# A two-layer hybrid trunk on one core: low halves of the first projection's weights moved from GpSimd to VectorE

## The chip, the cores and the metric

The kernel runs on one core of one Trainium2 chip. TensorE (PE) multiplies matrices, VectorE (DVE), ScalarE (ACT) and GpSimd (POOL) compute element by element, and SyncE (SP) issues the transfers. Each engine works through its own instructions in order; semaphores tie the engines together. The metric is the device time of one execution in microseconds (us).

## The reference

272 tokens (16 learned ones and 256 of input) with 1024 features go through two layers. Each layer is

```
h = x + W_out @ concat[ attention | RWKV-7 | convolution ]( RMSNorm(x) @ W_in )
x = h + PEER( RMSNorm(h) )
```

W_in has 2304 columns: 768 for the attention, 1024 for RWKV, 512 for the convolution. The RWKV part first mixes each token with the one before it (the token shift), and the convolution part is a gate and a depthwise filter of 31 taps:

```
prev = pad(z[:, :-1]);  z = z + (prev - z) * mu          # token shift
r, k, v, hw, ha, hg = split(z)
kk = k * k_k;  kk = kk * rsqrt(max(sum(kk * kk), 1e-12))
u = zc[..., :256] * sigmoid(zc[..., 256:])               # convolution's gate
u = conv(u, conv_w, 31 taps) + conv_b
```

PEER scores 128 x 128 experts by two sets of keys, keeps the top 16 of each head, and sums gated rows of two large tables (u and v, 16384 rows each).

## The kernel before, in words

**Weights in two halves.** All large products run in three passes for accuracy. A weight tile (128 x 1024, f32, 512 KB) is loaded by SP, copied by ACT to a rounded high half (`high`, L573), and the low half, weight minus high half, is computed by POOL (`low`, L495) or, for the v table alone, by DVE (L1548). TensorE then multiplies x_hi by w_hi, x_lo by w_hi and x_hi by w_lo (`tile`, 24 products). Tiles of a layer are numbered through: 0 to 17 the first projection (NZ = 18), 18 to 25 the output projection (NOUT = 8), 26 to 41 the query projection of PEER, then 128 tiles of u and 128 of v. Four slots (WR) form a ring: tile n can be loaded when TensorE has used tile n - 4, and ACT makes the high half of n + 2 (AHEAD) just before it waits for tile n to be used (`evacuate`).

**First projection.** Tile n of it gives 128 columns of z for all 272 tokens, and ACT copies them from PSUM (L597). Tiles 0 to 7 are RWKV's, 8 to 11 the convolution's, 12 to 17 the attention's. After tile 11 TensorE does six small products (the LoRAs) between tiles 11 and 12, for which it needs ACT's tanh and sigmoid of the token-shifted chunks 6 and 7; ACT then applies the gates (L653 to L662). The last of these, L662, releases the convolution.

**POOL's order in a layer** is written out: low halves up to tile 19 (`lows(l, 0 or 2, 20)`), then the convolution (one product L512, then 31 taps: two tensor_scalars L516 each, and an addition L525 from the second tap on), then low halves 20 to the end of u and the first two of v, and at last tiles 0 and 1 of the next layer.

**DVE's order in a layer:** the norm (`norm`), the token shift of eight chunks when tile 7 is evacuated (two operations each, L1269 and L1270), kk (L1279) and its square (L1280, the first request to TensorE), the decay (L1283), ten scans (L1288), L1290 to L1298, and L1300, which carries the second request to TensorE. TensorE answers both behind the projection, in order (`asked`), then runs 48 warm-up products on zeros, waits for the third request (L1318) and starts the transposes for the RWKV recurrence. Behind this come the recurrence and the attention, interleaved, and L1396, the request that ends them; TensorE waits for the convolution (`s_conv`) after it.

Of the kernel before, what the change touches and what calls it, by code (L numbers as in the profile page):

```python
# [26 lines left out]
ALU = mybir.AluOpType  # L27
ACT = mybir.ActivationFunctionType
AX = mybir.AxisListType
F32 = mybir.dt.float32  # L30
# [4 lines left out]
D = 1024  # L35
# [4 lines left out]
DEPTH = 2  # L40
# [6 lines left out]
NZ = 18  # L47
# [32 lines left out]
WR = 4  # L80
# [4 lines left out]
NW = NV0 + NKEYS  # L85
NP = NV0 + AHEAD
NLV = NW - NP
OHT = 4
UB = 4
PEEL = 2 * UB  # L90
# [113 lines left out]
def trunk(nc, h0, vec, res_c, mix_c, lora_c, keys_c, w_c, u_c, v_c, out):  # L204
    with ExitStack() as ctx:
# [9 lines left out]
        def sem(name):  # L215
            return ctx.enter_context(nc.semaphore(name))
# [135 lines left out]
        s_hi = sem("weights_high_ready")  # L352
        s_lo = sem("weights_low_ready")
        s_lv = sem("v_weights_low_ready")
        s_use = sem("weight_tile_used")
        s_sq = sem("squares_ready")
        s_ss = sem("square_sums_ready")
# [125 lines left out]
        @block.gpsimd  # L483
        def _(pool):
            nc.gpsimd.memset(zero_t[:, :], 0.0).then_inc(s_zero, 1)
            g = nc.gpsimd
            link = Link(pool, s_gl)

            def low(l, n, it=0):

                at = (l * NW + n) % WR * D
                slot = slice(at, at + D)

                pool.wait_ge(s_hi, l * NW + n + 1 + WR * it)  # L494
                g.tensor_tensor(wlo_t[:, slot], wraw_t[:, slot], whi_t[:, slot].bitcast(F32),  # L495
                                ALU.subtract).then_inc(s_lo, 1)

            def lows(l, n0, n1):

                whole = (n1 - n0) // WR  # L500
                with pool.Fori(0, whole) as it:  # L501
                    for j in range(WR):
                        low(l, n0 + j, it)
                for n in range(n0 + whole * WR, n1):
                    low(l, n)

            for l in range(DEPTH):
                lows(l, 0 if l == 0 else AHEAD, NZ + AHEAD)

                pool.wait_ge(s_cg, 2 * (l + 1))  # L510
                link(g.memset(cu[:, :, 0:CPAD], 0.0))
                link(g.tensor_tensor(cu[:, :, CPAD:CPAD + T], z[:, ZCU:ZCU + 2, 1:T + 1], cacc[:, :, :], ALU.mult))  # L512
                for k in range(CONV_K):
                    for j in range(2):
                        dst = cacc if k == 0 else ctmp
                        ins = g.tensor_scalar(dst[:, j, :], cu[:, j, k:k + T], vcol(l, "conv_w", j * CONV_K + k),  # L516
                                              vcol(l, "conv_b", j) if k == 0 else None, ALU.mult,
                                              *((ALU.add,) if k == 0 else ()))
                        if j == 0:
                            ins.then_inc(s_gl, 1)  # L520
                            link.n += 1
                        else:
                            link(ins)
                    if k:
                        ins = g.tensor_tensor(cacc[:, :, :], cacc[:, :, :], ctmp[:, :, :], ALU.add)  # L525
                        link(ins) if k < CONV_K - 1 else ins.then_inc(s_conv, 1)
                lows(l, NZ + AHEAD, NP)
                if l < DEPTH - 1:
                    for n in range(AHEAD):
                        low(l + 1, n)  # L530


        @block.scalar
# [246 lines left out]
        def _(pe):  # L780
# [21 lines left out]
            def tile(l, n, out_of, hi_of, lo_of, it=0):  # L802


                slot = (l * NW + n) % WR

                if n < NP:
                    pe.wait_ge(s_lo, l * NP + n + 1 + WR * it)
                else:
                    pe.wait_ge(s_lv, l * NLV + n - NP + 1 + WR * it)  # L810
                for c in range(DC):
                    for k, (a, b) in enumerate(((whi, hi_of), (whi, lo_of), (wlo, hi_of))):
                        last = mm(out_of(c), a[:, slot, c, :], b(c), c == 0 and k == 0, c == DC - 1 and k == 2)
                last.then_inc(s_use, 1)
# [70 lines left out]
            for l in range(DEPTH):  # L885
# [234 lines left out]
                def output(i, it=0):  # L1120
# [3 lines left out]
                    slot = (l * NW + n) % WR  # L1124

                    if n < NP:
                        pe.wait_ge(s_lo, l * NP + n + 1)
                    else:
                        pe.wait_ge(s_lv, l * NLV + n - NP + 1 + WR * it)
                    ah, al_ = act_hi[:, i % UB, 0:L.nt], act_lo[:, i % UB, 0:L.nt]  # L1130
# [17 lines left out]
        def _(dve):  # L1148
# [52 lines left out]
            def attention(l):  # L1201
# [23 lines left out]
                for n, s, q, nk, _ in groups(l):  # L1225
# [30 lines left out]
                    v.tensor_tensor(pr, pr, bc(rd, 2, nk), ALU.mult).then_inc(s_tn, 1)  # L1256
                    yield

            for l in range(DEPTH):
                if l == 0:  # L1260
                    dve.wait_ge(s_h, 48)
                L = LAYERS[l]
                norm(l, 0)
                dve.wait_ge(s_mix, 32 * (l + 1))
                link(v.memset(z[:, :, 0:1], 0.0))

                dve.wait_ge(s_ea, l * (NZ + NQ) + 8)
                for c in (6, 7, 0, 1, 2, 3, 4, 5):
                    link(v.tensor_tensor(t1[:, 0, :], z[:, c, 0:T], z[:, c, 1:T + 1], ALU.subtract))  # L1269
                    ins = v.scalar_tensor_tensor(zs[:, c, :], t1[:, 0, :], vcol(l, "mu", c), z[:, c, 1:T + 1],  # L1270
                                                 ALU.mult, ALU.add)
# [4 lines left out]
                        link(ins)  # L1276
                r_, k_, v_ = zs[:, 0:2, :], zs[:, 2:4, :], zs[:, 4:6, :]
                for j in range(2):
                    link(v.tensor_scalar(kk[:, j, :], k_[:, j, :], vcol(l, "k_k", j), None, ALU.mult))  # L1279
                ask_pe(v.tensor_tensor(t2[:, :, :], kk[:, :, :], kk[:, :, :], ALU.mult))  # L1280
                link(v.memset(lw[:, :, 0:PAD], 0.0))
# [346 lines left out]
```

## Time and profile before

| | |
|---|---|
| median of 3 runs | 2383.32 us (2376.61 to 2384.27) |
| profiled execution | 2378.84 us, span 2377.0 us |
| PE busy | 2188.9 us (92%) |
| DVE busy | 1400.2 us (59%) |
| ACT busy | 1032.4 us (43%) |
| POOL busy | 1075.3 us (45%) |
| POOL's low halves, L495 | 862.2 us for 344 |
| mean granted clock of TensorE | 0.953 |

Busy time is the union of an engine's instructions over the span, the time between the first and the last instruction. A granted clock of 1.00 is 2.4 GHz, 0.50 is 1.2 GHz. Two stretches of the span have a less busy TensorE: about 65 to 265 us, and 1285 to 1475 us. These are the mixing parts of the two layers, the region of the change.

### The profile page before, as it was taken

How to read it: one execution, taken by the hardware profiler on the slowest of the kernel's cores; microseconds unless marked ns; L12 is line 12 of the kernel's file. 1: busy time of each engine (PE TensorE's matmuls, PEld its weight loads, DVE VectorE, ACT ScalarE, POOL GpSimd, SP SyncE). 2: the span in 40 equal slices, each digit the busy share in tenths (PEclk: the TensorE clock that was granted, in tenths of full speed). 3: DMA queues.
4: the chain of work that ended last, by engine and by line, in shares of the span. 5: the costliest groups of instructions: out<-in, count | busy, mean ns of one | idle time of the engine just before them, and what ended most of it. 6: DMA issues, size and time to landing. Idle time of an engine off the chain costs nothing.

```text
span 2377.0 us, 49830 instructions
## 1 busy us (share of the span) xinstructions
PE 2188.9 (92%) x18763; PEld 2138.9 (90%) x18763; DVE 1400.2 (59%) x2846; ACT 1032.4 (43%) x1673; POOL 1075.3 (45%) x537
## 2 busy tenths in 40 slices
PE   7857799998999999999999667998999999999999
PEld 6855699998999999999989656898899999999999
DVE  2773318996667755555545844169527776555555
ACT  3412346664333344444445222466663333444444
POOL 4794356886666600000016981578876665000000
PEclk9866899999999999999999768999999999999999
DMA  4200244443433445555544000344444444555554
GB/s 154 82 2 1 71 144 141 160 160 124 135 137 133 133 159 176 172 174 175 176 139 145 16 1 28 133 169 159 168 166 142 142 139 140 185 185 184 185 185 168
DMA packets 88298, 320.11 MB, mean 135 GB/s; under 512 B 9744, under 2 KB 11024, under 8 KB 87824
## 3 DMA queue, kind: packets, MB, share of 16 engines
q1 hardware_dynamic: 88208, 318.91, 39.5%
q8 instruction: 57, 0.93, 0.2%
q14 instruction: 33, 0.27, 0.0%
HBM read 317.82 MB, written 1.05 MB: 134 GB/s over the span
## 4 chain that ended last, share of the span: by engine, by line
PE 57%; POOL 22%; issue 19%; DVE 1%; ACT 0%; POOLq 0%; DMA 0%; SPq 0%; DVEq 0%
PE ps L782 57%; POOL w_lo L495 14%; POOL arena L516 5%; POOL arena L525 3%; DVE h L1566 0%; POOLq L501 0%; DMA w<-w_c 0%; DVE x L1188 0%; POOL arena L512 0%; POOLq L494 0%; DVE x_lo L1181 0%; DVE sel L1478 0%; ACT arena L591 0%; DVE onehots_j L1176 0%; PE ps L1108 0%
## 5 line engine op out<-in xcount | busy, mean ns | idle before, releaser
L782 PE MATMUL ps<-x_hi,w_hi 128*128 128x272 f32 (+1 forms) x6816 | 1542.9, 287 | 43.8 <-POOL w_lo L495 29.6
L782 PE MATMUL ps<-x_hi,w_lo 128*128 128x272 f32 (+1 forms) x4768 | 1361.0, 285 | 0.0
L495 POOL TENSOR_TENSOR w_lo<-w,w_hi 128x1024 fp32r<-128x1024 f32 x344 | 862.2, 2515 | 920.1 <-ACT w_hi L573 919.6
L782 PEld LDWEIGHTS ps<-x_hi,w_hi 128*128 128x128 f32 x6816 | 1150.8, 189 | 52.2 <-POOL w_lo L495 36.3
L782 PEld LDWEIGHTS ps<-x_hi,w_lo 128*128 128x128 f32 x4768 | 900.4, 189 | 0.0
L573 ACT CAST w_hi<-w 128x1024 fp32r<-128x1024 f32 x596 | 623.1, 1046 | 440.1 <-DMA w<-v_c 393.2
L782 PE MATMUL ps<-x_lo,w_hi 128*128 128x272 f32 (+1 forms) x2720 | 777.3, 286 | 0.0
L782 PEld LDWEIGHTS ps<-x_lo,w_hi 128*128 128x128 f32 x2720 | 515.2, 189 | 0.2
L1548 DVE TENSOR_TENSOR w_lo<-w,w_hi 128x1024 fp32r<-128x1024 f32 x252 | 308.8, 1225 | 342.3 <-ACT w_hi L573 342.3
L782 PE MATMUL ps<-arena 64*64 64x64 f32 (+7 forms) x2432 | 183.3, 285 | 85.2 <-ACT arena L688 21.2
L782 PEld LDWEIGHTS ps<-arena 64*64 64x64 f32 (+5 forms) x2432 | 153.6, 179 | 113.2 <-issue 30.5
L754 ACT ACTIVATE arena<-ps 128x272 f32<-128x272 f32 (+43 forms) x132 | 37.2, 282 | 319.5 <-PE ps L782 319.5
L782 PE MATMUL ps<-onehots_i,onehots_j 128*128 128x128 f32 x1056 | 139.1, 274 | 1.0 <-DVE onehots_i L1502 1.0
L782 PEld LDWEIGHTS ps<-onehots_i,onehots_j 128*128 128x128 f32 x1056 | 129.4, 191 | 1.4 <-DVE onehots_i L1502 1.4
L516 POOL TENSOR_SCALAR arena<-arena,vecs 128x272 f32<-128x272 f32 x124 | 127.2, 1037 | 6.1
L1511 DVE TENSOR_TENSOR arena<-arena,ps 128x4 f32<-128x4 f32 (+43 forms) x130 | 37.9, 292 | 140.4 <-ACT ps L756 140.4
L1539 DVE TENSOR_TENSOR x_hi<-arena,x_hi 128x272 fp32r<-128x272 f32 (+1 forms) x256 | 108.9, 426 | 1.0 <-ACT x_hi L763 1.0
L763 ACT CAST x_hi<-arena 128x272 fp32r (+3 forms) x256 | 104.1, 407 | 2.3 <-DVE arena L1521 2.3
L736 ACT ACTIVATE arena<-ps 128x256 f32 (+2 forms) x124 | 48.5, 391 | 126.9 <-PE ps L782 126.3
L1437 DVE MAX8 arena<-arena 128x8 f32<-128x128 f32 (+3 forms) x120 | 29.5, 320 | 106.2 <-ACT arena L727 105.9
L1495 DVE TENSOR_TENSOR ps<-ps,sel 128x512 f32<-128x512 f32 x132 | 91.0, 689 | 0.0
L1502 DVE TENSOR_TENSOR onehots_i<-ps,sel 128x512 f32<-128x512 f32 x132 | 90.2, 683 | 0.3
(152 smaller groups left out, 1454.4 us busy)
## 6 DMA issues: line engine op xcount, KB each, us to landing
w<-u_c SPq DMA_DIRECT2D x256, 512.0 KB, 3.2
w<-v_c SPq DMA_DIRECT2D x256, 512.0 KB, 3.2
w<-w_c SPq DMA_DIRECT2D x84, 512.0 KB, 3.2
arena<-keys_c SPq DMA_DIRECT2D x2, 1024.0 KB, 6.3
arena<-mix_c SPq DMA_DIRECT2D x2, 632.0 KB, 6.7
h<-h SPq DMA_DIRECT2D x1, 1088.0 KB, 5.0
out<-h SPq DMA_DIRECT2D x4, 256.0 KB, 2.3
arena<-lora_c SPq DMA_DIRECT2D x2, 256.0 KB, 6.9
```

Of the source, the lines that this page charges most:

```text
L495: g.tensor_tensor(wlo_t[:, slot], wraw_t[:, slot], whi_t[:, slot].bitcast(F32), ALU.subtract).then_inc(s_lo, 1)
L516: ins = g.tensor_scalar(dst[:, j, :], cu[:, j, k:k + T], vcol(l, "conv_w", j * CONV_K + k), vcol(l, "conv_b", j) if k == 0 else None, ALU. ...
L525: ins = g.tensor_tensor(cacc[:, :, :], cacc[:, :, :], ctmp[:, :, :], ALU.add)
L573: nc.scalar.copy(whi_t[:, slot * D:(slot + 1) * D], wraw_t[:, slot * D:(slot + 1) * D]).then_inc(s_hi, 1)
L736: nc.scalar.activation(hid[l][:, bass.ds(WR * it + (i0 + j), 1), :].squeeze(1), ps[:, 1 + (i0 + j) % UB, 0:L.nt], ACT.Gelu_apprx_tanh).the ...
L763: nc.scalar.copy(act_hi[:, i % UB, 0:L.nt], hid[l][:, bass.ds(WR * it + i, 1), :].squeeze(1)).then_inc(s_ah, 1)
L782: return nc.tensor.matmul(out_, lhsT, rhs, start=start, stop=stop, skip_group_check=True)
L1495: v.tensor_tensor(eq, iota_ps, bc(sel[:, 1, g:g + OHT], 2, P), ALU.is_equal).then_inc(s_dl, 1)
L1502: v.tensor_tensor(ohA[:, k % 2], eq, bc(sel[:, 0, g:g + OHT], 2, P), ALU.mult).then_inc(s_oh, 1)
L1511: v.tensor_tensor(row, row, ps[:, 1 + (L.split + k) % UB, 0:OHT * k], ALU.mult).then_inc(s_hm, 1)
L1539: v.tensor_tensor(act_lo[:, i % UB, 0:L.nt], hid[l][:, bass.ds(WR * it + i, 1), :].squeeze(1), act_hi[:, i % UB, 0:L.nt].bitcast(F32), ALU ...
L1548: v.tensor_tensor(wlo_t[:, slot], wraw_t[:, slot], whi_t[:, slot].bitcast(F32), ALU.subtract).then_inc(s_lv, 1)
```

## The change

DVE computes the low halves of tiles 0 to 19 of each layer, with a semaphore of their own, `s_lz`, for TensorE to wait on. Two stand before the norm, eight behind it (EARLY = 10), one ahead of each of the eight token-shift pairs, and one ahead of each of the two kk operations. POOL begins each layer with the convolution and goes on with tile 20. The counts that TensorE waits for on `s_lo` are shifted to match.

```diff
+EARLY = 10
@@ POOL
             for l in range(DEPTH):
-                lows(l, 0 if l == 0 else AHEAD, NZ + AHEAD)
-
                 pool.wait_ge(s_cg, 2 * (l + 1))
...
                 lows(l, NZ + AHEAD, NP)
-                if l < DEPTH - 1:
-                    for n in range(AHEAD):
-                        low(l + 1, n)
@@ TensorE, tile
-                if n < NP:
-                    pe.wait_ge(s_lo, l * NP + n + 1 + WR * it)
+                if n < NZ + AHEAD:
+                    pe.wait_ge(s_lz, l * (NZ + AHEAD) + n + 1)
                 else:
-                    pe.wait_ge(s_lv, l * NLV + n - NP + 1 + WR * it)
+                    pe.wait_ge(s_lo, l * (NP - NZ - AHEAD) + n - NZ - AHEAD + 1 + WR * it)
@@ DVE
+            def projection_low(l, n):
+
+                at = (l * NW + n) % WR * D
+                slot = slice(at, at + D)
+                dve.wait_ge(s_hi, l * NW + n + 1)
+                v.tensor_tensor(wlo_t[:, slot], wraw_t[:, slot], whi_t[:, slot].bitcast(F32),
+                                ALU.subtract).then_inc(s_lz, 1)
...
                 L = LAYERS[l]
+                for n in range(AHEAD):
+                    projection_low(l, n)
                 norm(l, 0)
                 dve.wait_ge(s_mix, 32 * (l + 1))
                 link(v.memset(z[:, :, 0:1], 0.0))
 
+                for n in range(AHEAD, EARLY):
+                    projection_low(l, n)
                 dve.wait_ge(s_ea, l * (NZ + NQ) + 8)
-                for c in (6, 7, 0, 1, 2, 3, 4, 5):
+                for i, c in enumerate((6, 7, 0, 1, 2, 3, 4, 5)):
+                    projection_low(l, EARLY + i)
                     link(v.tensor_tensor(t1[:, 0, :], z[:, c, 0:T], z[:, c, 1:T + 1], ALU.subtract))
...
                 for j in range(2):
+                    projection_low(l, EARLY + 8 + j)
                     link(v.tensor_scalar(kk[:, j, :], k_[:, j, :], vcol(l, "k_k", j), None, ALU.mult))
```

On DVE, from the last two pairs of the token shift to the scans and what follows them, there stood before (w, w_hi and w_lo are a weight tile and its halves, arena is the working memory):

```order
L1269 TENSOR_TENSOR arena<-arena 128x272
L1270 SCALAR_TENSOR_TENSOR arena<-arena,vecs 128x272
L1269 TENSOR_TENSOR arena<-arena 128x272
L1270 SCALAR_TENSOR_TENSOR arena<-arena,vecs 128x272
L1279 TENSOR_SCALAR arena<-arena,vecs 128x272 x2
L1280 TENSOR_TENSOR arena<-arena 128x544
L1281 MEMSET arena 128x2x48
L1283 TENSOR_SCALAR arena<-arena 128x2x272
L1288 SCALAR_TENSOR_TENSOR arena<-res,arena 128x64 x10
L1290 TENSOR_TENSOR arena<-arena 128x640
```

and now, where L1261 is the low half and L1279, L1280, L1290 and L1299 are the token shift, kk and the scans of before:

```order
L1261 TENSOR_TENSOR w_lo<-w,w_hi 128x1024
L1279 TENSOR_TENSOR arena<-arena 128x272
L1280 SCALAR_TENSOR_TENSOR arena<-arena,vecs 128x272
L1261 TENSOR_TENSOR w_lo<-w,w_hi 128x1024
L1290 TENSOR_SCALAR arena<-arena,vecs 128x272
L1261 TENSOR_TENSOR w_lo<-w,w_hi 128x1024
L1290 TENSOR_SCALAR arena<-arena,vecs 128x272
L1291 TENSOR_TENSOR arena<-arena 128x544
L1292 MEMSET arena 128x2x48
L1294 TENSOR_SCALAR arena<-arena 128x2x272
L1299 SCALAR_TENSOR_TENSOR arena<-res,arena 128x64 x10
L1301 TENSOR_TENSOR arena<-arena 128x640
```

Low halves 17, 18 and 19 stand in these rows: every operation from the scans on stands behind the low half of tile 19.

On POOL, layer 0, at the turn from the low halves to the convolution, there stood before:

```order
L494 REGISTER_ALU
L495 TENSOR_TENSOR w_lo<-w,w_hi 128x1024 [waits weights_high_ready]
L494 REGISTER_ALU
L495 TENSOR_TENSOR w_lo<-w,w_hi 128x1024 [waits weights_high_ready]
L501 REGISTER_ALU
L501 COMPARE_AND_BRANCH
L511 MEMSET arena 128x2x30 [waits conv_gate_ready]
L512 TENSOR_TENSOR arena<-arena 128x2x272 [waits pool_link]
L516 ISA
```

and now at the start of the layer:

```order
L487 MEMSET zeros 128x128
L511 MEMSET arena 128x2x30 [waits conv_gate_ready]
L512 ISA
L512 TENSOR_TENSOR arena<-arena 128x2x272 [waits pool_link]
L516 TENSOR_SCALAR arena<-arena,vecs 128x272 [waits pool_link]
L516 TENSOR_SCALAR arena<-arena,vecs 128x272
L516 TENSOR_SCALAR arena<-arena,vecs 128x272 [waits pool_link]
```

The convolution now waits for its gate alone (conv_gate_ready), with nothing of the layer in front of it.

## Rows read from the trace of the kernel before

**Rows 1.** The page: chain that ended last; costliest groups (busy us, mean ns).
```profile
PE ps L782 57%; POOL w_lo L495 14%; POOL arena L516 5%; POOL arena L525 3%; DVE h L1566 0%; POOLq L501 0%; DMA w<-w_c 0%; DVE x L1188 0%; POOL arena L512 0%; POOLq L494 0%; DVE x_lo L1181 0%; DVE sel L1478 0%; ACT arena L591 0%; DVE onehots_j L1176 0%; PE ps L1108 0%
...
L495 POOL TENSOR_TENSOR w_lo<-w,w_hi 128x1024 fp32r<-128x1024 f32 x344 | 862.2, 2515 | 920.1 <-ACT w_hi L573 919.6
...
L1548 DVE TENSOR_TENSOR w_lo<-w,w_hi 128x1024 fp32r<-128x1024 f32 x252 | 308.8, 1225 | 342.3 <-ACT w_hi L573 342.3
```

**Rows 2.** Waits of TensorE, 305 to 600 us: total us, times, longest.
```profile
PE ps L782 <- POOL w_lo L495: 15.6, 13, 7.3
```

**Rows 3.** Time line of TensorE, layer 0: start us, us, engine, line, operation.
```profile
97.88 2.18 PE L782 MATMUL ps<-arena 128*128 128x272 f32 x4 [3.76 <-DVE arena L1300]
99.85 12.58 PE L782 MATMUL ps<-zeros 128*128 128x128 f32 x96
112.36 3.71 PE L782 MATMUL ps<-res,arena 64*64 64x64 f32 x120
...
250.88 2.15 PE L782 MATMUL ps<-arena,res 128*128 128x272 f32 x4 [7.90 <-DVE arena L1396]
```

**Rows 4.** Time line of DVE, layer 0.
```profile
70.95 0.76 DVE L1279 TENSOR_SCALAR arena<-arena,vecs 128x272 f32<-128x272 f32 x2
71.75 0.72 DVE L1280 TENSOR_TENSOR arena<-arena 128x544 f32<-128x544 f32 x1
...
76.42 0.44 DVE L1283 TENSOR_SCALAR arena<-arena 128x544 f32<-128x544 f32 x1 [3.84 <-ACT arena L659]
76.90 11.57 DVE L1288 TENSOR_TENSOR_SCAN arena<-res,arena 128x64 f32<-128x64 f32 x10
...
90.15 4.21 DVE L1295 TENSOR_SCALAR arena<-arena,vecs 128x272 f32<-128x272 f32 x2
94.40 1.71 DVE L1296 SCALAR_TENSOR_TENSOR arena<-arena 128x544 f32<-128x544 f32 x1
...
96.77 1.05 DVE L1300 SCALAR_TENSOR_TENSOR arena<-arena,vecs 128x272 f32<-128x272 f32 x2
...
103.72 1.75 DVE L1309 TENSOR_TENSOR arena<-arena 128x544 f32<-128x544 f32 x1
...
107.90 1.86 DVE L1317 TENSOR_TENSOR arena<-arena 128x544 f32<-128x544 f32 x1
109.79 0.90 DVE L1318 TENSOR_TENSOR arena<-arena 128x544 f32<-128x544 f32 x1
```

**Rows 5.** Time line of POOL, layer 0.
```profile
77.98 7.20 POOL L495 TENSOR_TENSOR w_lo<-w,w_hi 128x1024 fp32r<-128x1024 f32 x3 [11.43 <-ACT w_hi L573]
...
94.28 1.24 POOL L512 TENSOR_TENSOR arena<-arena 128x544 f32<-128x544 f32 x1
95.64 3.96 POOL L516 TENSOR_SCALAR arena<-arena,vecs 128x272 f32<-128x272 f32 x4
...
205.01 1.33 POOL L525 TENSOR_TENSOR arena<-arena 128x544 f32<-128x544 f32 x1
```

**Rows 6.** Line 1288, the scans, 76 to 89 us: ns min/median/max.
```profile
L1288 DVE TENSOR_TENSOR_SCAN arena<-res,arena x10: 291/292/2456, 76.9 to 88.2; 128x64 f32<-128x64 f32 x10
```

**Rows 7.** Time line of ACT, layer 0.
```profile
76.17 0.80 ACT L662 ACTIVATE arena<-arena 128x272 f32<-128x272 f32 x2
...
90.49 1.05 ACT L573 CAST w_hi<-w 128x1024 fp32r<-128x1024 f32 x1
```

**Rows 8.** Line 597, evacuations of tiles 12 to 17, 78 to 95 us.
```profile
L597 ACT COPY arena<-ps x6: 386/386/389, 78.1 to 93.2; 128x272 f32<-128x272 f32 x6
```

**Rows 9.** Stretches: us, busy us by engine, then granted clock, DMA share, GB/s.
```profile
99.80:102.00 2.20, 2.20 (x12) 2.15 (x11) 2.20 (x1) 2.19 (x4) 2.10 (x2) 0.50 0.00 0
104.00:106.00 2.00, 2.00 (x20) 2.00 (x19) 1.93 (x3) 0.00 (x0) 1.90 (x2) 1.00 0.00 0
```

**Rows 10.** Time line of ACT, layer 1.
```profile
1305.91 1.05 ACT L573 CAST w_hi<-w 128x1024 fp32r<-128x1024 f32 x1
```

**Rows 11.** Time line of DVE, layer 1.
```profile
1311.64 1.06 DVE L1300 SCALAR_TENSOR_TENSOR arena<-arena,vecs 128x272 f32<-128x272 f32 x2
```

More of the change, by code:

```diff
@@ L354, in trunk @@
         s_lv = sem("v_weights_low_ready")
+        s_lz = sem("first_projection_weights_low_ready")
         s_use = sem("weight_tile_used")
@@ L1126, in output @@
                     if n < NP:
-                        pe.wait_ge(s_lo, l * NP + n + 1)
+                        pe.wait_ge(s_lo, l * (NP - NZ - AHEAD) + n - NZ - AHEAD + 1)
                     else:
```

## The prediction

> **What bounds the kernel now.** I read the page first, then who waited for whom on TensorE, then the time lines of the four engines around the first projection. Three things are to be seen.
>
> First, TensorE never waits for a low half in this projection. Its only waits on POOL's L495 are in the stretch 305 to 600 us (15.6 us) and its counterpart in layer 1, where POOL computes the low halves of peer_wq and u [rows 1, 2]; the change leaves those where they are. Taking 18 slow subtractions from POOL (2.515 us each against 1.225 for the same shape on DVE [rows 1]) therefore buys TensorE nothing by itself.
>
> Second, what TensorE waits for behind the projection is DVE: 3.8 us for L1300, the last operation before the second request to TensorE [rows 3]. DVE comes to it late because of POOL. After the last token-shift operation DVE does L1279 to L1281 by 72.6 us, waits for ACT until 76.42, and needs 21.4 us from there to the end of L1300 (96.77 + 1.05 = 97.82) [rows 4]. In that stretch POOL runs low halves, from 77.98 until shortly before the convolution's product at 94.28 [rows 5], and whole DVE instructions stand still behind them: ten scans with a median of 0.292 us take 11.57 us together, one of them 2.456 [rows 4, 6].
>
> Third, TensorE does its two products at 97.88, then the 48 warm-up products (99.85, 12.58 us), and starts the RWKV transposes at 112.36; DVE's request for these was there at 109.79 + 0.90 = 110.69 [rows 3, 4]. So the stage starts 14.54 us after the end of L1300, with 1.67 us of slack on DVE's side. A delay of L1300 goes through in full.
>
> **The convolution does not end last.** Its first instruction with data runs at 94.28 and its last ends at 206.34 [rows 5]. TensorE uses it only after the wait for L1396, the request that ends the RWKV part, 7.9 us [rows 3], which lies behind 250 us. The convolution thus has some 44 us to spare.
>
> **The change part by part.**
>
> (a) POOL loses 20 low halves in layer 0 and 18 in layer 1, and the two of layer 1 at the end of layer 0. The convolution starts when its gate is there (ACT's L662 ends at 76.97 [rows 7]) and not just before 94.28: 17 us earlier, ending near 189. With 44 us of slack that is worth 0 directly.
>
> (b) Low halves 0 and 1 stand before the norm on DVE, 2 x 1.23 = 2.5 us. DVE is idle there, waiting for the squares' sum and the root; cost 0. If that cover went, 2.5 us per layer. Low halves 2 to 9 fall in the time in which DVE is idle for TensorE's first eight tiles: 0. Low halves 10 to 17 between the token shifts: tile 14 has its high half when ACT is through the gates (about 77.9), and each one after follows 3.03 us later, TensorE's pace (six tiles evacuated from 78.1 to 93.2 [rows 8]). A low half and a shift are 1.23 + 1.0 = 2.2 us, which fits under 3.03, so TensorE is fed: 0. If POOL's blocks took that cover, about 0.5 us per tile over four tiles.
>
> (c) The cost: DVE is in order, and kk now stands behind low halves 18 and 19. The high half of tile 19 is ready at 90.49 + 1.05 = 91.54 [rows 7]. Low half 19 then runs to 91.6 + 1.2 = 92.8, the second kk to 93.2 (0.38 each [rows 4]), the square takes 0.72 [rows 4] and the memset about 0.1: L1283 starts at 94.05 instead of 76.42. Before, all of this was done at 72.6 and only ACT was waited for; that work now hides nothing, because it stands behind the last weights.
>
> (d) What is saved in the stretch L1283 to L1300, now free of POOL's low halves. Scans: 11.57 minus ten of about 0.32 with their gap, 8.3 us. L1295: 4.21 minus 0.76, as L1279 of the same shape takes for two: 3.4. L1296: 1.71 minus 0.72, as the two-input L1280 of the same size takes: 1.0 [rows 4]. So 21.4 - 12.7 = 8.7 us undisturbed, and L1300 would end at 94.05 + 8.7 = 102.8.
>
> (e) But the convolution now lies over this stretch. Its two-input additions block DVE too: L1296 waited for the product at 94.28, and L1309 and L1317 took 1.75 and 1.86 us where L1280 and L1318, of the same size, take 0.72 and 0.90 [rows 4, 5]. Its tensor_scalars do not: both L1300 ran in 1.05 together in the middle of the four at 95.64 [rows 4, 5]. One addition comes about every 3.4 to 4 us. Over 10 to 12 us these are three blocks, at most 1.3 us each, some 1.1 typically: 3.3 us. Bounds: 0 if all fall under memsets and copies, 5 if a fourth one hits and low half 19 is caught as well. I take 3.3, because the stretch 94 to 112 shows three in about this density. L1300 ends at 106.1: 8.3 us later than 97.82.
>
> (f) Layer 1 by the same steps: the high half of tile 19 at 1305.91 + 1.05 = 1306.96 [rows 10]; plus 0.07, 1.2, 0.4 and 0.83 gives 1309.5; plus 8.7 and 3.3 gives 1321.5, against 1311.64 + 1.06 = 1312.70 [rows 11]: 8.8 us.
>
> (g) The convolution ends some 17 us earlier while the RWKV chain runs 8 us later, so the last 25 us of what it covered are free of it. The chain there waits mostly for TensorE; a block or so on the way to the softmax is saved: 0 to 2 us per layer, I take 0.5.
>
> (h) TensorE idles some 11 us before L1300 and not 3.8. After the 3.8 us the granted clock is 0.50 (1.2 GHz), still so from 99.80 to 102.00, and 1.00 (2.4 GHz) from 104 [rows 9]. A longer wait starts from the same low level and the same work follows, so I take 0; bound: if the clock stayed low through the 48 warm-ups, see the rivals.
>
> Sum: 8.3 + 8.8 - 1.0 = 16.1 us. The profiled execution took 2378.84 us, so 2394.9 by its own measure. It lies 4.5 us below the median shown, 2383.32, within runs of 2376.61 to 2384.27; I forecast 2397, between the two references (2394.9 and 2399.4). The difference to the median is then +0.6%.
>
> **A rule weighed.** The rows say: POOL's one-input tensor_scalars left L1300 alone, 1.05 us for two [rows 4, 5]. The Trainium skill, "SBUF — State Buffer", section "Who interferes with whom", says that a DVE instruction with two SBUF inputs contends with any GpSimd instruction that reads SBUF, and that the first to come holds the shared pair for its whole length. By that rule the tensor_scalars would block as well, and the sum would be that of rival 3. For the two-input operations of POOL the rule and the scans agree.
>
> **Rivals.**
> 1. Faster: the convolution is the last to end before the output projection (the page's chain runs through L516 and L525, 5% and 3% [rows 1]), and starting 17 us earlier takes up to 17 us off each layer: 2379 - 34 = 2345. It decides if the convolution ends after the request of L1396, behind 250 us. Against: it ended at 206.34 [rows 5], and from there the chain only goes back along POOL's own order. Chance 0.05.
> 2. No measurable difference: no block by the convolution (L1300 at 102.8 and 1318.2, so +5.0 and +5.5) and full relief at the tail, 2 us each: +6.5, 2385 by the profile's measure. For: the phase of the additions is luck. Against: three blocks in the like stretch of before. Chance 0.09.
> 3. Every operation of the convolution blocks: the 16 two-port operations of the stretch wait about 0.9 us each, 14 us and not 3.3. 16 + 2 x 11 = +38, 2417. Against: the L1300 rows. Chance 0.05.
> 4. The clock stays at 1.2 GHz longer. In the stretch at 0.50 twelve products were started in 2.2 us, at 1.00 twenty in 2.0 [rows 9]: 96 at the low rate are 17.6 us and not 12.6, 5 us per layer: 2405. Chance 0.09.
> The forecast has 0.72.
>
> **Numbers.** The forecast's own range is 2388 to 2404. To leave no more than 2 in 10 out it reaches towards rivals 2 and 4: 2387 to 2408. What this kernel can tell from no change is about 0.3%, 7 us: faster 0.05 (rival 1), same 0.09 (rival 2), slower 0.86.
>
> **What would show it.** In the profile after: TensorE's wait for the second product's request grows from 3.8 to about 11 us in each layer (the wait for the first one, on the square, stays near 1); the scans take 3 to 6 us and not 11.6, and start near 94.5; the convolution starts near 77 and ends near 189 to 192; the projection's tiles still come every 3.03 us; the stage after the warm-ups starts near 120.6. I am wrong if TensorE waits for the square and low halves within the projection, if the warm-up is short enough to absorb the delay, if the scans are blocked as before, or if the time from the transposes to the output projection changes by more than 2 us.

## The result, and the profile after

| | before | changed |
|---|---|---|
| median | 2379.76 us (9 runs, 2370.87 to 2384.27) | 2391.78 us (9 runs, 2383.88 to 2402.77) |
| ratio | | 1.006, 95% interval 1.0038 to 1.0083 |
| profiled execution | 2378.84 us, span 2377.0 | 2391.78 us, span 2389.9 |
| POOL busy | 1075.3 us | 994.6 us |
| DVE busy | 1400.2 us | 1424.7 us |

The changed kernel is 12 us slower (0.6%), inside the range and with the sign that was forecast. In the changed kernel every line name moves: the low half on DVE is L1261, kk and its square L1290 and L1291, the decay L1294, the scans L1299, L1306 to L1311 are L1295 to L1300 of before, and L1329 is the third request (L1318). The page's chain and POOL's low halves, 40 fewer of them:

```profile
PE ps L779 58%; POOL w_lo L497 12%; POOL arena L516 6%; POOL arena L525 3%; DMA arena<-lora_c 0%; DVE h L1577 0%; DVE x L1185 0%; DVE x_lo L1178 0%; DVE onehots_j L1173 0%; POOLq L503 0%; ACT L647 0%; ACT L646 0%; POOL arena L512 0%; DVE sel L1489 0%; POOLq L496 0%
...
L497 POOL TENSOR_TENSOR w_lo<-w,w_hi 128x1024 fp32r<-128x1024 f32 x304 | 767.0, 2533 | 483.4 <-ACT w_hi L570 483.1
```

DVE in layer 0: low half 14, the first one behind the LoRAs, then from low half 19 to the third request (start, us, engine, line, operation; it answers to [rows 4]):

```profile
80.37 1.59 DVE L1261 TENSOR_TENSOR w_lo<-w,w_hi 128x1024 fp32r<-128x1024 f32 x1 [11.41 <-ACT w_hi L570]
...
93.76 2.01 DVE L1261 TENSOR_TENSOR w_lo<-w,w_hi 128x1024 fp32r<-128x1024 f32 x1 [0.84 <-ACT w_hi L570]
95.69 0.58 DVE L1290 TENSOR_SCALAR arena<-arena,vecs 128x272 f32<-128x272 f32 x1
96.31 0.73 DVE L1291 TENSOR_TENSOR arena<-arena 128x544 f32<-128x544 f32 x1
...
97.18 0.51 DVE L1294 TENSOR_SCALAR arena<-arena 128x544 f32<-128x544 f32 x1
97.72 5.87 DVE L1299 TENSOR_TENSOR_SCAN arena<-res,arena 128x64 f32<-128x64 f32 x10
...
105.27 1.71 DVE L1306 TENSOR_SCALAR arena<-arena,vecs 128x272 f32<-128x272 f32 x2
107.01 0.97 DVE L1307 SCALAR_TENSOR_TENSOR arena<-arena 128x544 f32<-128x544 f32 x1
...
108.60 2.06 DVE L1311 SCALAR_TENSOR_TENSOR arena<-arena,vecs 128x272 f32<-128x272 f32 x2
...
122.63 0.90 DVE L1329 TENSOR_TENSOR arena<-arena 128x544 f32<-128x544 f32 x1
```

At 80.37 DVE has stood idle for 11.41 us, waiting for the high half of tile 14, with token shifts still to do that were done by 70.9 us before. Low half 19 starts at 93.76, when ACT has its high half, and all that stood at 70.95 to 76.42 before now stands behind it. The decay starts at 97.18 and not 76.42. The scans take 5.87 us and not 11.57, L1306 1.71 and not 4.21. The second request's operation ends at 108.60 + 2.06 = 110.66; it was 97.82. In layer 1 it ends at 1325.33, where it was 1312.70 [rows 11]:

```profile
1323.27 2.06 DVE L1311 SCALAR_TENSOR_TENSOR arena<-arena,vecs 128x272 f32<-128x272 f32 x2
```

The scans one by one, ns min/median/max (before 291/292/2456 [rows 6]):

```profile
L1299 DVE TENSOR_TENSOR_SCAN arena<-res,arena x10: 290/301/1466, 97.7 to 103.0; 128x64 f32<-128x64 f32 x10
```

The longest wait is now 1.2 us, one addition of the convolution, and not 2.2 us, one low half. TensorE in the same stretch (it answers to [rows 3]; each of these products stands in the rows as two matmuls, so x96 are the 48 warm-up products):

```profile
97.19 1.16 PE L779 MATMUL ps<-arena 128*128 128x272 f32 x4 [1.87 <-DVE arena L1291]
110.72 2.18 PE L779 MATMUL ps<-arena 128*128 128x272 f32 x4 [12.38 <-DVE arena L1311]
112.69 12.19 PE L779 MATMUL ps<-zeros 128*128 128x128 f32 x96
124.81 3.71 PE L779 MATMUL ps<-res,arena 64*64 64x64 f32 x120
```

It waits 1.87 us for the square, and 12.38 us for L1311 where it waited 3.76. Before, it had the square at once, right behind the last tile:

```profile
93.04 1.08 PE L782 MATMUL ps<-arena 128*128 128x272 f32 x4
```

From L1311's end to the transposes it is 14.15 us, before 14.54. POOL, start and end of the convolution (it answers to [rows 5]):

```profile
79.62 1.26 POOL L512 TENSOR_TENSOR arena<-arena 128x544 f32<-128x544 f32 x1
80.99 6.78 POOL L516 TENSOR_SCALAR arena<-arena,vecs 128x272 f32<-128x272 f32 x4
```

```profile
196.44 2.49 POOL L525 TENSOR_TENSOR arena<-arena 128x544 f32<-128x544 f32 x1
268.91 4.76 POOL L497 TENSOR_TENSOR w_lo<-w,w_hi 128x1024 fp32r<-128x1024 f32 x2 [69.99 <-ACT w_hi L570]
```

It starts at 79.62 and ends at 198.93, then POOL idles for 70 us: the earlier convolution brings nothing. The four tensor_scalars at 80.99 take 6.78 us and not 3.96: DVE now computes low halves beside them. The tiles of the projection still come every 3.03 us (80.2 to 95.4 for six, as in [rows 8]), and TensorE waits in 60 to 96 us for nothing but the tanh and sigmoid:

```profile
L594 ACT COPY arena<-ps x6: 386/388/391, 80.2 to 95.4; 128x272 f32<-128x272 f32 x6
```

```profile
PE ps L779 <- ACT arena L647: 4.1, 1, 4.1
```

**Where the 12.9 us of the two spans are.** The changed execution enters the projection later: its first tile is evacuated at 34.8 us and not 32.5, mostly because TensorE's clock rose to 2.4 GHz later there (from 30 to 33 us the granted clock was 0.52, and the products start 0.225 us apart and not 0.125). Whether the change has a part in these 2.3 us is not settled. Of the ten profiles of the experiments below five have this tile at 32.2 to 32.7 and five at 34.1 to 35.1, and spread and spread_late_conv, which are alike up to there, stand on different sides, so the order of the instructions does not decide it. But with the first two profiles all three of kernels with the order of before are on the early side, and six of the nine with low halves on DVE on the late one. Then layer 0 gives back nearly all of its delay in the recurrence, and layer 1 nothing; what lies behind the two mixing parts took 0.9 and 2.4 us less than before. The stretch from ACT's first copy of the transposes to the output projection, after and before (us, busy us of PE, PEld, DVE, ACT, POOL, then granted clock, DMA share, GB/s):

```profile
125.80:272.00 146.20, 94.64 (x1364) 81.44 (x1361) 80.75 (x154) 38.31 (x111) 72.49 (x64) 0.78 0.01 1
1340.70:1492.20 151.50, 101.80 (x1324) 85.81 (x1321) 77.63 (x138) 35.08 (x90) 71.39 (x63) 0.71 0.01 1
```

```profile
113.30:269.50 156.20, 103.08 (x1366) 87.67 (x1363) 82.79 (x154) 38.31 (x111) 91.39 (x81) 0.70 0.01 1
1328.30:1476.90 148.60, 98.71 (x1326) 84.24 (x1323) 78.48 (x138) 35.08 (x90) 90.93 (x81) 0.71 0.00 1
```

In layer 0 it takes 146.2 us and not 156.2, at a granted clock of 0.78 and not 0.70; in layer 1 151.5 and not 148.6, at 0.71 in both. So the first pair of profiles left open whether the change shortens the recurrence of one layer, or whether this was the granted clock of that execution.

### The profile page after: what moved, and what is told of

The parts are those of the page before. It is cut to its first block, busy times and chain, and to the rows that moved or that the text cites. A ratio compares the mean times of both kernels' runs of the same rounds, so it can differ in the third digit from the quotient of the medians.

```text
span 2389.9 us, 49784 instructions
## 1 busy us (share of the span) xinstructions
PE 2184.3 (91%) x18763; PEld 2134.8 (89%) x18763; DVE 1424.7 (60%) x2886; ACT 1033.0 (43%) x1673; POOL 994.6 (42%) x497
## 4 chain that ended last, share of the span: by engine, by line
PE 58%; POOL 21%; issue 18%; DVE 1%; ACT 1%; DMA 0%; POOLq 0%; SPq 0%
PE ps L779 58%; POOL w_lo L497 12%; POOL arena L516 6%; POOL arena L525 3%; DMA arena<-lora_c 0%; DVE h L1577 0%; DVE x L1185 0%; DVE x_lo L1178 0%; DVE onehots_j L1173 0%; POOLq L503 0%; ACT L647 0%; ACT L646 0%; POOL arena L512 0%; DVE sel L1489 0%; POOLq L496 0%
## 5 line engine op out<-in xcount | busy, mean ns | idle before, releaser
L497 POOL TENSOR_TENSOR w_lo<-w,w_hi 128x1024 fp32r<-128x1024 f32 x304 | 767.0, 2533 | 483.4 <-ACT w_hi L570 483.1
L1559 DVE TENSOR_TENSOR w_lo<-w,w_hi 128x1024 fp32r<-128x1024 f32 x252 | 308.8, 1225 | 343.1 <-ACT w_hi L570 343.1
L516 POOL TENSOR_SCALAR arena<-arena,vecs 128x272 f32<-128x272 f32 x124 | 138.9, 1132 | 6.1
L733 ACT ACTIVATE arena<-ps 128x256 f32 (+2 forms) x124 | 48.5, 391 | 127.2 <-PE ps L779 126.3
L1261 DVE TENSOR_TENSOR w_lo<-w,w_hi 128x1024 fp32r<-128x1024 f32 x40 | 52.6, 1319 | 75.2 <-ACT w_hi L570 74.9
```

The costliest lines, as they stand in the source:

```text
L733: nc.scalar.activation(hid[l][:, bass.ds(WR * it + (i0 + j), 1), :].squeeze(1), ps[:, 1 + (i0 + j) % UB, 0:L.nt], ACT.Gelu_apprx_tanh).the ...
L1261: v.tensor_tensor(wlo_t[:, slot], wraw_t[:, slot], whi_t[:, slot].bitcast(F32), ALU.subtract).then_inc(s_lz, 1)
L1559: v.tensor_tensor(wlo_t[:, slot], wraw_t[:, slot], whi_t[:, slot].bitcast(F32), ALU.subtract).then_inc(s_lv, 1)
```

## The experiments

Times are medians; each ratio is to runs of the kernel before on the same chip. For all of them one table is worked out from the time lines of their profiles, in us, layer 0 / layer 1: (A) the end of the second request's operation (L1300 or its like) minus the end of the last evacuation of the projection, (B) from there to ACT's first copy of the transposes, (C) from there to the first addition of the output projection, and their sum.

| kernel | A | B | C | A + B + C |
|---|---|---|---|---|
| before | 4.2 / 3.7 | 15.5 / 15.6 | 156.2 / 148.6 | 175.9 / 167.9 |
| before_again | 4.1 / 4.9 | 15.6 / 15.7 | 152.4 / 148.6 | 172.0 / 169.2 |
| changed | 14.9 / 14.8 | 15.1 / 15.3 | 146.2 / 151.6 | 176.2 / 181.7 |
| after_again | 15.0 / 13.5 | 15.0 / 14.2 | 151.9 / 150.4 | 181.9 / 178.1 |
| fill | 14.9 / 14.9 | 13.9 / 13.9 | 153.3 / 149.0 | 182.1 / 177.8 |
| late_two | 9.7 / 9.6 | 14.3 / 14.4 | 148.7 / 150.8 | 172.7 / 174.7 |
| spread | 1.3 / 1.2 | 13.9 / 13.9 | 150.4 / 149.5 | 165.7 / 164.6 |
| spread_again | 1.2 / 1.4 | 13.9 / 13.9 | 151.3 / 151.5 | 166.4 / 166.8 |
| spread_late_conv | -3.6 / -3.7 | 16.7 / 16.7 | 156.3 / 147.6 | 169.3 / 160.6 |
| before_one_tap | 4.2 / 4.2 | 15.5 / 15.4 | 148.2 / 144.2 | 167.8 / 163.8 |
| after_one_tap | 9.0 / 9.0 | 14.7 / 14.9 | 148.8 / 143.9 | 172.5 / 167.8 |
| after_no_add | 9.7 / 9.7 | 15.3 / 14.3 | 148.6 / 142.8 | 173.6 / 166.8 |

### The same two kernels again: after_again, before_again

No edit.

> The changed kernel once more. Theory A (the delay of L1311 is systematic, 12 to 13 us in each layer, and what the first profile gave back in layer 0 was the granted clock's luck): L1311 again ends about 12 us later than L1300 did, relative to the projection's end, in both layers; the time from the first transposes to the output projection differs from the first profile by several us in at least one layer, and goes with the granted clock of that stretch. Time 0.4 to 0.9% above before. Theory B (something in the changed order shortens layer 0's recurrence): it is again 10 us shorter than before in layer 0 and not in layer 1.

> The kernel before once more, for a second profile. Theory A: L1300 ends within 1 us of 4.6 us behind the last evacuation of the projection in both layers, and the time from the first transposes to the output projection varies by several us with the granted clock. Theory B: it is the same as in the first profile within 1 us.

Measured: 2391.24 us, ratio 1.007 (1.0042 to 1.0098), and 2369.90 us for the single run of before. A repeats within 1.4 us and separates the kernels: 13.5 to 15.0 against 3.7 to 4.9. That is 9 to 11 us and not the 12 to 13 expected, which had the late entry into the projection in it. C does not separate them: layer 0 took 151.9 us in the second profile of the changed kernel and 152.4 in the second one of before. The 10 us that layer 0 gave back are gone, and with them the case for theory B: no shortening of the recurrence by 10 us repeats. Smaller ones stay below the scatter of C. Both kernels spread over 10 us or more between executions, and it goes with the mean granted clock: the nine runs of the changed kernel lie between 2402.77 us at a mean granted clock of 0.947 and 2383.88 us at 0.958.

### Only the last two low halves moved: late_two

```diff
                 for j in range(2):
-                    projection_low(l, EARLY + 8 + j)
                     link(v.tensor_scalar(kk[:, j, :], ...))
...
                 v.tensor_tensor(sq[:, 0:5, :], ...).then_inc(s_q2, 1)
+                for j in range(2):
+                    projection_low(l, EARLY + 8 + j)
```

> The changed kernel with low halves 18 and 19 moved behind the third request (after L1331), where DVE waits for TensorE. Theory A (the cost is that kk and all behind it wait for the last weights): kk starts when the shift behind low half 17 ends, about 91.5 in the first profile's time and not 95.7, so L1311 ends some 4 us earlier in each layer, 8 us in all: 2384 against before's 2380. Rival (the cost is DVE's extra work and the convolution's blocks): the two low halves take 2.5 us and that is all that can come back, 2 us per layer.

Measured: 2382.16 us, ratio 1.0022 (1.0005 to 1.004), 9.1 us below after_again on the same chip. DVE in layer 0, from low half 17 to the second request:

```profile
87.57 1.96 DVE L1261 TENSOR_TENSOR w_lo<-w,w_hi 128x1024 fp32r<-128x1024 f32 x1 [0.76 <-ACT w_hi L570]
...
90.48 0.87 DVE L1289 TENSOR_SCALAR arena<-arena,vecs 128x272 f32<-128x272 f32 x2
...
92.25 1.38 DVE L1293 TENSOR_SCALAR arena<-arena 128x544 f32<-128x544 f32 x1
93.67 4.61 DVE L1298 TENSOR_TENSOR_SCAN arena<-res,arena 128x64 f32<-128x64 f32 x10
...
102.50 2.06 DVE L1310 SCALAR_TENSOR_TENSOR arena<-arena,vecs 128x272 f32<-128x272 f32 x2
```

kk starts at 90.48, and A falls from 14.9 to 9.7 and from 14.8 to 9.6, by 5 us per layer (by 5.3 and 3.9 from after_again). Measured from the last evacuation, the decay starts 4.0 us earlier in layer 0 (-2.6 us and not 1.4), as theory A had it. Two low halves are 2.5 us of work, so more came back than the work: in the changed kernel DVE had also waited 0.84 us for the high half of tile 19, and low half 19 and the kk behind it had been held 1.0 us by the convolution. The last 1.2 us of the 5 lie behind the decay (12.31 us to the end of the second request and not 13.48, the scans 4.61 and not 5.87): the additions fall otherwise on the chain, which is luck of their phase. In after_again, with the low halves in their old place, layer 1 has these 4.61 us for the scans too.

### All low halves where DVE has time: spread

```diff
                 for i, c in enumerate((6, 7, 0, 1, 2, 3, 4, 5)):
-                    projection_low(l, EARLY + i)
+                    if i < 4:
+                        projection_low(l, EARLY + i)
...
                         link(v.tensor_tensor_scan(cum[:, j, w], ...))
+                        if NCH * j + c in (2, 6, 9):
+                            projection_low(l, EARLY + {2: 4, 6: 5, 9: 6}[NCH * j + c])
...
                     link(v.memset(a[:, :, 0:PAD], 0.0))
+                projection_low(l, EARLY + 7)
```

with low halves 18 and 19 as in late_two.

> The changed kernel with the token shift freed: low halves 10 to 13 before the first four shifts, 14 to 16 between the scans, 17 ahead of L1306, 18 and 19 behind the third request. Theory A: the decay starts at about 76.5 as before, L1311's end falls to 93 to 96 us (97.8 before), TensorE waits 0 to 2 us for it at the full clock, so the 48 warm-ups take 9.6 to 12 us, and the stage starts 2 to 5 us earlier than in before: 2370 to 2376. Rival (moving the low halves to DVE costs whatever their place, since DVE is the engine TensorE waits for): 4 x 1.23 us of low halves stand in the chain plus three blocks by the convolution, L1311 ends at 98 or later, time not below before.

Measured: 2366.45 us, ratio 0.9962 (0.9942 to 0.9982), and once more as spread_again 2371.32 us, 0.9972 (0.9954 to 0.999). Faster than before both times: with the same work on DVE, its place alone turns 1.006 and 1.007 into 0.996 and 0.997. (2370 to 2376 had been expected beside 2380 for before, which are ratios of 0.996 to 0.998.) DVE in layer 0:

```profile
76.11 0.45 DVE L1294 TENSOR_SCALAR arena<-arena 128x544 f32<-128x544 f32 x1 [3.98 <-ACT arena L656]
76.59 1.82 DVE L1299 TENSOR_TENSOR_SCAN arena<-res,arena 128x64 f32<-128x64 f32 x3
78.44 1.25 DVE L1261 TENSOR_TENSOR w_lo<-w,w_hi 128x1024 fp32r<-128x1024 f32 x1
...
92.53 2.08 DVE L1314 SCALAR_TENSOR_TENSOR arena<-arena,vecs 128x272 f32<-128x272 f32 x2
...
106.57 0.89 DVE L1332 TENSOR_TENSOR arena<-arena 128x544 f32<-128x544 f32 x1
```

The decay starts at 76.11 as before, the low halves stand between the scans, and L1314 ends at 94.61, 1.3 us behind the last evacuation. From the decay to there it is 18.5 us where before had 21.4: four low halves on DVE, 6.2 us with what holds them, cost this chain less than POOL's had. TensorE:

```profile
94.66 1.19 PE L779 MATMUL ps<-arena 128*128 128x272 f32 x4 [0.91 <-DVE arena L1314]
95.68 10.88 PE L779 MATMUL ps<-zeros 128*128 128x128 f32 x96
107.52 3.71 PE L779 MATMUL ps<-res,arena 64*64 64x64 f32 x120 [0.96 <-DVE arena L1332]
```

It waits 0.91 us for the second request at full clock, the warm-ups take 10.88 us and not 12.58, and now DVE's third request comes last (0.96). The rival of this run, that low halves on DVE cost whatever their place, falls.

> The kernel spread once more, for the comparison: L1314's end 1.2 to 1.3 us behind the last evacuation, the stage 13.9 us behind that, ratio to before 0.994 to 0.998.

As expected, but for 1.4 us in layer 1 (A) where 1.2 to 1.3 stood.

### The convolution's price: after_one_tap, before_one_tap, after_no_add

```diff
-                for k in range(CONV_K):
+                for k in range(1):
```

in both kernels (the last instruction then signals s_conv), and in after_no_add, with all 62 tensor_scalars kept:

```diff
-                    if k:
+                    if k == CONV_K - 1:
                         ins = g.tensor_tensor(cacc[:, :, :], cacc[:, :, :], ctmp[:, :, :], ALU.add)
```

> The changed kernel without taps 2 to 31 of the convolution (this part of the computation is left out), so that POOL is silent from about 85 us on. Theory A (the convolution's additions took what the undisturbed sum of 8.7 us lacks): from the start of the decay to the end of L1311 8.7 to 9.5 us and not 13.5, and L1311 ends 9 to 10 us behind the last evacuation and not 14.9. Rival (the low halves on DVE or something else slow the stretch): it stays near 13 us. Against before_one_tap still 5 to 6 us per layer slower.

> The kernel before without taps 2 to 31 of the convolution (left out). Theory A: the scans still take 11.5 us since POOL's low halves block them; L1300 ends 3 to 4 us behind the last evacuation; the recurrence is 1 to 4 us shorter per layer than before. So the changed kernel's extra cost without the convolution is 5 to 6 us per layer at L1300, where with it it is 10 to 11.

> The changed kernel with the convolution's tensor_scalars all kept and its additions of taps 2 to 30 left out (30 of 31 taps are not summed). Theory A (only POOL's two-input operations block DVE): decay to L1311's end 8.7 to 10 us, as in after_one_tap. Rival (any POOL instruction that reads SBUF blocks DVE's two-input instructions): 20 us or more, since POOL is never silent then; each scan would wait up to 0.95 us.

Measured: after_one_tap 2370.61 us, 0.9958 (0.9936 to 0.9979); before_one_tap 2366.39 us, 0.9941 (0.992 to 0.9962); after_no_add 2370.91 us, one run. after_one_tap, DVE, and its scans:

```profile
95.90 0.45 DVE L1290 TENSOR_SCALAR arena<-arena 128x544 f32<-128x544 f32 x1
...
101.28 0.76 DVE L1302 TENSOR_SCALAR arena<-arena,vecs 128x272 f32<-128x272 f32 x2
...
103.42 1.03 DVE L1307 SCALAR_TENSOR_TENSOR arena<-arena,vecs 128x272 f32<-128x272 f32 x2
```

```profile
L1295 DVE TENSOR_TENSOR_SCAN arena<-res,arena x10: 291/291/293, 96.4 to 99.3; 128x64 f32<-128x64 f32 x10
```

From the decay's start (95.90) to L1307's end (104.45) it is 8.55 us (8.7 to 9.5 was expected), in the changed kernel 97.18 to 110.66, 13.48. So the convolution costs this stretch 4.9 us, and A another 1.0 ahead of it (0.4 and not 1.3 to 1.5 from the last evacuation to the decay): 5.9 of A's 14.9. Without the convolution A differs by 4.8 us per layer between the two kernels, with it by 10.3 (means of the two profiles each): theory A, a little under the 5 to 6 forecast. A + B + C differs by 8.7 us over both layers there, the medians by only 4.2; six runs each, spread over 5 and 9 us, do not settle which. In before_one_tap the scans still take 11.5 us, L1300 ends 4.2 us behind the last evacuation (3 to 4 was expected), and C is 4.4 us shorter in layer 1 and 4 to 8 in layer 0 than with the convolution, more than the 1 to 4 expected. In the changed kernel C of layer 1 is 6.5 to 7.7 us shorter without the convolution, while C of layer 0 (148.8 against 146.2 and 151.9) stays within its scatter. So over the recurrence, too, the convolution costs several microseconds, shown for layer 1: all nine profiles with it have 147.6 to 151.6 us there, the three without it or its additions 142.8 to 144.2. For layer 0 (146.2 to 156.3 against 148.2 to 148.8) it is not shown. That it is the additions that cost this is likely but not shown either: after_no_add is as low, but its tensor_scalars end at 152.3, early in the recurrence. after_no_add:

```profile
78.37 72.68 POOL L516 TENSOR_SCALAR arena<-arena,vecs 128x272 f32<-128x272 f32 x61
```

```profile
98.78 0.79 DVE L1306 TENSOR_SCALAR arena<-arena,vecs 128x272 f32<-128x272 f32 x2
...
100.94 1.22 DVE L1311 SCALAR_TENSOR_TENSOR arena<-arena,vecs 128x272 f32<-128x272 f32 x2
```

```profile
L1299 DVE TENSOR_TENSOR_SCAN arena<-res,arena x10: 291/292/396, 93.7 to 96.8; 128x64 f32<-128x64 f32 x10
```

POOL never pauses between 78.37 and 151, 61 tensor_scalars in a row, and yet the longest scan is 0.396 us, L1306 takes 0.79 and not 1.71, and A is 9.7, 0.7 above after_one_tap. The stretch from the decay to the end of the second request takes 9.00 us: of the 4.9 us that the convolution costs it, the additions make 4.5 and the tensor_scalars 0.45. So only POOL's two-input operations hold DVE up whole; its tensor_scalars cost DVE 0.1 to 0.25 us here and there. The rival of 20 us or more falls, and with it rival 3 of the prediction. The tensor_scalars do meet DVE, but it is POOL that pays: between 78 and 112 us they take up to 2.19 us, the longest of them beside DVE's low halves, and 0.96 us beside a reciprocal of DVE, which has one input:

```profile
L516 POOL TENSOR_SCALAR arena<-arena,vecs x26: 743/1052/2190, 78.4 to 111.4; 128x272 f32<-128x272 f32 x26
```

```profile
L516 POOL TENSOR_SCALAR arena<-arena,vecs x4: 963/964/964, 103.4 to 106.3; 128x272 f32<-128x272 f32 x4
```

### The idle time filled: fill

```diff
                 last.then_inc(s_pd, 1)
 
+                pe.wait_ge(s_ea, l * (NZ + NQ) + NZ)
+                warm(56, 1)
                 asked()
```

> The changed kernel with 56 more warm-up products on TensorE between the first and the second request, where it idles 12.4 us. Theory A (the clock's part of the cost is small, since DVE's third request comes 12.9 us behind L1311 anyway): the second product and the 48 warm-ups run at 2.4 GHz, 1.1 and 9.6 to 11 us, the stage starts 14 us and not 15.1 behind L1311's end: 2 to 3 us in all, 2388. Rival (the idle time costs through the clock of the whole stage): 8 us or more come back, 2382 or below.

Measured: 2388.27 us, ratio 1.004 (1.0023 to 1.0057). TensorE in layer 0:

```profile
98.50 12.67 PE L779 MATMUL ps<-zeros 128*128 128x128 f32 x112
111.06 1.19 PE L779 MATMUL ps<-arena 128*128 128x272 f32 x4
112.08 10.88 PE L779 MATMUL ps<-zeros 128*128 128x128 f32 x96
123.92 3.71 PE L779 MATMUL ps<-res,arena 64*64 64x64 f32 x120 [0.96 <-DVE arena L1331]
```

The second product takes 1.19 us and not 2.18, the 48 warm-ups 10.88 and not 12.19, and then TensorE waits 0.96 us for DVE. B is 13.9 and not 15.1 and 15.3 (15.0 and 14.2 in after_again): 1.1 us per layer in the mean, 2 us in all. The medians are 3.0 and 3.5 us apart, but the kernels did not run side by side; the ratios, 1.004 against 1.006 and 1.007, are 5 to 7 us apart with overlapping intervals, so the times by themselves do not decide between the theories. The profiles do: A, which is DVE's, is unchanged, and C (153.3 and 149.0) is no shorter than in the changed kernel, so nothing of the rival's 8 us is to be found in the stage. Theory A: the clock is the small part.

### The convolution held back: spread_late_conv

```diff
                 pool.wait_ge(s_cg, 2 * (l + 1))
+                pool.wait_ge(s_st, NCH * l + 1)
```

on top of spread.

> The kernel spread, with the convolution held back until the third request is made (POOL also waits for the memset of the state behind it). Theory A (the convolution's additions cost the chain ahead of the stage 5 us up to L1314 and 2.5 behind it, and it has 50 us to spare): the chain runs undisturbed, the third request comes 10.4 us behind the second one and not 12.9, TensorE's 48 warm-ups then end last, and the stage starts 12 to 12.5 us behind the last evacuation and not 15.2: 2 to 3 us per layer. The convolution ends near 222 us in layer 0, 20 us ahead of its need, and its last 30 us fall on the recurrence. Ratio to before 0.992 to 0.996. Rival (blocks are only moved: what the prologue saves the recurrence loses): no change against spread, 0.996.

Measured: 2368.19 us, ratio 0.9945 (0.9926 to 0.9963), beside spread_again at 0.9972 on the same chip; the intervals overlap, so a gain over spread is likely but not shown.

```profile
94.94 2.00 PE L780 MATMUL ps<-arena 128*128 128x272 f32 x8
96.78 10.88 PE L780 MATMUL ps<-zeros 128*128 128x128 f32 x96
107.59 3.72 PE L780 MATMUL ps<-res,arena 64*64 64x64 f32 x120
```

```profile
107.01 2.17 POOL L513 TENSOR_TENSOR arena<-arena 128x544 f32<-128x544 f32 x1
```

A falls to -3.6: L1315 is done before the projection is. But then TensorE is the later one: it takes both products and the warm-ups back to back from 94.94 to 107.59, so A + B is 13.0 (12 to 12.5 was expected) where spread has 15.2: 2.2 us per layer, the low end of the 2 to 3 expected. Neither theory is cleanly right: C was 156.3 and 147.6 us, which its scatter of some 5 us does not tell from spread's.

## Why the prediction was right, step by step

- **The path.** Right: the second request is what TensorE waits for (12.38 us), its delay goes through (B is 15.1 and 15.3 against 15.5 and 15.6), TensorE waits for no low half in the projection, and the convolution ends at 198.93, 54 us before TensorE starts on L1407's request at 253.36, ahead of its own use. Rival 1 is refuted: POOL's work shrank, the convolution ended 7 us earlier, and the time rose. One detail was wrong: the wait for the square was to stay near 1 us; it was none before and is 1.87 us now.
- **(a).** Right that it is worth nothing directly, wrong in size: the convolution was to end near 189 to 192 us and ended at 198.93, as it started 2.6 us later than forecast (2 us of this by the late entry) and its tensor_scalars took longer, 138.9 us for the 124 and not 127.2.
- **(b).** Right: the tiles keep their pace of 3.03 us. The two low halves ahead of the norm cost nothing that can be seen: spread has them there too and starts its first product at 28.84 us, before at 29.15.
- **(c), (d).** Right in size, shown by after_one_tap: from the last evacuation to the decay 0.4 us, from the decay to the end of the second request 8.55 us, where the sum had 0.4 and 8.7.
- **(e).** Mis-sized. I took 3.3 us for three blocks and 5 as the bound; it is 4.9 in the stretch and 1.0 ahead of it (low half 19 2.01 us and not 1.23, kk 0.58 and not 0.36), 5.9 in all and beyond the bound. Layer 1 of after_again, the mildest of the four, has 3.7 and 0.8. In the changed kernel four of the convolution's additions fall in the stretch: two in the scans, one at L1306, one at L1311. DVE works there nearly back to back and meets each of them, while the stretch from which I took the density, three blocks in 18 us, has a reciprocal of 3.55 us with one input under which one addition passed unseen. So A rose by 10.3 us (mean of two profiles) and not by 8.3 and 8.8.
- **(g), (h).** Too small. B shrank by 0.7 us and C, in the mean of two profiles, by 1.4 us per layer, where I had 0.5 for both. For C this is argued only: its single values scatter by 10 us.
- **The sum.** A + B + C rose from a mean of 171.3 to 179.5 us, 8.2 us per layer and 16.5 in all, against 16.1 forecast. That this agrees so well is luck: A rose by 1.8 us more per layer than forecast, and B and C gave back 1.6 us more, two errors that cancelled. The medians give 12.0 and, in the second series, 15.7 us; one execution of either kernel can be 5 to 10 us off, along with its mean granted clock. The first profile would have read as no loss in layer 0 (0.3 us) and 13.8 in layer 1, both wrong as measures of the change. By the prediction's own sign of being wrong (the time from the transposes to the output projection changes by more than 2 us) the first pair spoke against it, with 10 us less and 3 us more; the second pair has 0.5 us less and 1.8 us more, so the sign was set tighter than two executions of one kernel agree.
- **Rivals 2 to 4.** Rival 2 needed no blocks; only after_one_tap has none, and there A's rise is 4.8 us per layer, as rival 2 had it (5.0 and 5.5). Rival 3 fell with after_no_add. Rival 4: the warm-ups took 12.19 us, the clock rose as early as before.

What stays open is why C of layer 0 varies between 146 and 156 us. The granted clock of the stretch goes with it only in part (0.78 with 146.2 and 0.70 with 156.2 us, but 0.71 with 151.9 in after_again and 0.72 with 156.3 in spread_late_conv), and no run fixed the clock.

## What to carry to other kernels

In an in-order engine the price of inserted work is its length and, on top, the wait in front of it. Ten low halves, some 12 us of work, stood one by one ahead of the token shift and kk; they had to wait for weights that come every 3 us, and the decay behind them moved from 76.42 to 97.18 us, 2 us of this by the late entry. Taking only the last two out won back 4.0 us ahead of the decay for 2.5 us of work; with the low halves in places where their weights are there, the same twenty cost nothing (A 1.3 us and not 4.2). Before moving work off an engine that blocks another, list what then slides into its place: the low halves' blocks left the stretch from the decay to the second request (21.4 us before, 8.55 us free of POOL), and the convolution's took 5.9 of these 12.9 us back. And a profile pair of two executions is not enough for a change of half a per cent; compare the distance between two events that the change touches over several profiles.

## What the runs showed of the hardware

- POOL's two-input additions held DVE's two-input instructions (scans, tensor_tensor, scalar_tensor_tensor) and its tensor_scalars for up to 1.2 us of an addition's 1.34: a scan of 0.29 us took 1.47, two L1306 1.71 and not 0.76. POOL's tensor_scalars held them by 0.1 to 0.25 us at most (scans 0.291 to 0.396 us under 61 of them in a row, two L1311 1.22 us and not 1.03). The Trainium skill, "SBUF — State Buffer", section "Who interferes with whom", has a DVE instruction with two SBUF inputs contend with a GpSimd instruction that reads SBUF. The additions here agree. For the tensor_scalars the measurement agrees that they meet, since POOL's side is longer for it, but DVE is never held for the length of one.
- The other way round POOL's tensor_scalars are held by DVE: four of them took 6.78 us beside DVE's low halves and 3.96 without, and in after_no_add single ones took up to 2.19 us and not 0.96.
- After 12.38 us of idling TensorE's clock came back as soon after the work resumed as after 3.76 us: 48 warm-ups took 12.19 and 12.58 us.
